# Four attentions in a two-block transformer: the product of the values ahead of the turn of the next probabilities

## The reference, cut to what matters

```python
s = q @ k.T * scale + mask         # 128 x (128, 256 or 512) scores
p = softmax(s, axis=-1)            # maximum, exp, sum, division
o = p @ v                          # 128 values (64 in the dilated one)
```

## Time and profile before

| | us |
|---|---|
| median of 3 runs | 1654.51 |
| lowest and highest run | 1649.87, 1654.61 |
| the profiled execution, its own time | 1649.54 |
| its span | 1647.8 |
| PE busy in it | 1546.7 (94%) |
| DVE, ACT busy | 1133.9 (69%), 796.8 (48%) |

### The profile page before, as it was taken

How to read it: one execution, slowest core, us unless ns; L and a number is a source line. 1 busy time by engine, 2 the same in 40 slices (tenths; PEclk the granted TensorE clock), 3 DMA queues, 4 the chain that set the end, 5 groups by cost and what they waited for, 6 DMA issues and landing times.

```text
span 1647.8 us, 31024 instructions
## 1 busy us (share of the span) xinstructions
PE 1546.7 (94%) x11438; PEld 1364.2 (83%) x11438; DVE 1133.9 (69%) x1901; ACT 796.8 (48%) x1437; POOL 124.6 (8%) x139
## 2 busy tenths in 40 slices
PE   5899988899899999999899999999999889999998
PEld 3688878888677777788786699999898669999997
DVE  5976866554799999867545468885665765577654
ACT  3545553242544444422355457774445455566532
POOL 2000152512000000001000010001000001000000
PEclk9999999999899999999899999999899999999999
DMA  9345510002255555554342035556454214255552
GB/s 364 112 174 179 187 46 1 3 2 77 96 186 180 189 185 184 178 179 153 118 148 77 1 128 191 180 195 212 152 167 141 90 65 130 89 192 187 183 191 89
DMA packets 62955, 230.77 MB, mean 140 GB/s; under 512 B 6800, under 2 KB 8080, under 8 KB 62352
## 3 DMA queue, kind: packets, MB, share of 16 engines
q1 hardware_dynamic: 61408, 223.37, 40.1%
q0 software_dynamic: 1168, 5.80, 1.0%
q10 hardware_dynamic: 288, 0.33, 0.1%
HBM read 228.43 MB, written 1.05 MB: 139 GB/s over the span
## 4 chain that ended last, share of the span: by engine, by line
PE 80%; DVE 11%; ACT 4%; issue 3%; POOL 1%; DMA 1%; DVEq 0%; ACTq 0%; POOLq 0%
PE proj L646 22%; PE proj L648 21%; PE proj L647 21%; DVE w_low L2138 2%; PE bank L698 1%; PE bank L900 1%; ACT w_high L1625 1%; PE bank L920 1%; PE bank L917 1%; DVE conv_mid L2218 1%; DMA ident_sb<-ident 1%; PE proj L1122 1%; DVE h_low L2171 1%; DVE tmp L2182 1%; PE bank L706 1%
## 5 line engine op out<-in xcount | busy, mean ns | idle before, releaser
L646 PE MATMUL proj<-h_high,w_high 128*128 128x256 f32 (+1 forms) x1776 | 584.7, 329 | 24.6 <-DVE h_low L2171 14.5
L648 PE MATMUL proj<-h_high,w_low 128*128 128x256 f32 (+1 forms) x1776 | 571.3, 322 | 0.0
L647 PE MATMUL proj<-h_low,w_high 128*128 128x256 f32 (+1 forms) x1776 | 570.4, 321 | 0.0
L2138 DVE TENSOR_TENSOR w_low<-w_raw,w_high 128x1024 fp32r<-128x1024 f32 x322 | 393.5, 1225 | 178.2 <-ACT w_high L1625 177.1
L1625 ACT ACTIVATE w_high<-w_raw 128x1024 fp32r<-128x1024 f32 x322 | 338.2, 1054 | 231.8 <-PE proj L648 227.5
L646 PEld LDWEIGHTS proj<-h_high,w_high 128*128 128x128 f32 x1776 | 336.8, 190 | 67.7 <-issue 19.1
L648 PEld LDWEIGHTS proj<-h_high,w_low 128*128 128x128 f32 x1776 | 337.2, 190 | 26.9
L647 PEld LDWEIGHTS proj<-h_low,w_high 128*128 128x128 f32 x1776 | 337.0, 190 | 24.6
L646 PE MATMUL proj<-act_high,w_high 128*128 128x256 f32 (+1 forms) x608 | 190.4, 313 | 0.4 <-DVE w_low L2138 0.4
L648 PE MATMUL proj<-act_high,w_low 128*128 128x256 f32 (+1 forms) x608 | 189.6, 312 | 0.0
L647 PE MATMUL proj<-act_low,w_high 128*128 128x256 f32 (+1 forms) x608 | 188.9, 311 | 0.0
(11 more groups left out here) (408 smaller groups left out, 1890.1 us busy)
## 6 DMA issues: line engine op xcount, KB each, us to landing
w_raw<-w_stream SPq DMA_DIRECT2D x322, 512.0 KB, 3.3
a_ring<-a_stream SPq DMA_DIRECT2D x80, 512.0 KB, 3.2
a_first<-a_head SPq DMA_DIRECT2D x4, 1024.0 KB, 18.1
a_first<-a_stream SPq DMA_DIRECT2D x4, 1024.0 KB, 18.6
x<-x_in SPq DMA_DIRECT2D x1, 2048.0 KB, 10.5
late_tab<-late_tables POOLq DMA_DIRECT2D x1, 1408.0 KB, 6.8
cond_rows<-cond_rows SPq DMA_DIRECT2D x1, 1024.0 KB, 5.9
cond_rows<-cond_rows POOLq DMA_DIRECT2D x1, 1024.0 KB, 5.2
```

Source lines behind the costliest of these rows:

```text
L646: mm(out_, wh, xh, start=first, stop=False)
L647: mm(out_, wh, xl, start=False, stop=False)
L648: return mm(out_, wl, xh, start=False, stop=last)
L2138: v.tensor_tensor(wl(n), RAW[:, n % 4, :], wh(n), ALU.subtract).then_inc(w_low, 1)
```

## The change

In both functions that write PE's part of an attention step, the block of the product with the values (of step a - 3) now stands ahead of the block of the turn (of step a - 2). Nothing else is altered: each block keeps its waits and its signals, and the lists of ACT, DVE, POOL and SP are the same as before. With the lines moved, the turn has the numbers L1172 and L1204 in the new kernel.

```diff
--- before.py
+++ after.py
@@ -1157,12 +1157,6 @@
                         elif ly is not MLA:
                             pe.wait_ge(A["at_p"], ly.a0 + max(0, a - nb + 1))
                             scores(a // 2, a % 2, ly.banks[a % nb]).then_inc(A["at_s"], 1)
-                    if 2 <= a < ly.n + 2:
-                        p = a - 2
-                        pe.wait_ge(A["at_n"], ly.a0 + p + 1)
-                        for k in range(ly.kt):
-                            last = nc.tensor.transpose(BK[2 + p % 2][:, k * P:(k + 1) * P], PB[:, p % 3, k * P:(k + 1) * P], ID[:])
-                        last.then_inc(A["at_t"], 1)
                     if a >= 3:
                         p = a - 3
                         pe.wait_ge(A["at_pt"], ly.a0 + p + 1)
@@ -1171,6 +1165,12 @@
                             pe.wait_ge(A["at_y"], ly.e0 + e - 1)
                         h, qt = (p // 4 * 2 + p % 2, p // 2 % 2) if ly is MLA else (p // 2, p % 2)
                         values(h, qt, PT[:, p % 2, :, :]).then_inc(A["at_o"], 1)
+                    if 2 <= a < ly.n + 2:
+                        p = a - 2
+                        pe.wait_ge(A["at_n"], ly.a0 + p + 1)
+                        for k in range(ly.kt):
+                            last = nc.tensor.transpose(BK[2 + p % 2][:, k * P:(k + 1) * P], PB[:, p % 3, k * P:(k + 1) * P], ID[:])
+                        last.then_inc(A["at_t"], 1)
 
             def pair_step(ly, a, scores, values):
 
@@ -1180,15 +1180,6 @@
                     for i in range(2):
                         last = scores(ly.pairs[a // 2][i], a % 2, BK[a % 2][:, i * SEQ:i * SEQ + (1 + a % 2) * P])
                     last.then_inc(A["at_s"], 1)
-                if 2 <= a < ly.n + 2:
-                    p = a - 2
-                    nk = 1 + p % 2
-                    pe.wait_ge(A["at_n"], ly.a0 + p + 1)
-                    for i in range(2):
-                        for k in range(nk):
-                            at = i * SEQ + k * P
-                            last = nc.tensor.transpose(BK[2 + p % 2][:, (i * nk + k) * P:(i * nk + k + 1) * P], PB[:, p % 3, at:at + P], ID[:])
-                    last.then_inc(A["at_t"], 1)
                 if 3 <= a < ly.n + 3:
                     p = a - 3
                     e, nk = p // 2, 1 + p % 2
@@ -1203,6 +1194,15 @@
                     for i in range(2):
                         last = values(ly.pairs[e][i], p % 2, PT[:, p % 2, i * nk:(i + 1) * nk, :], nk)
                     last.then_inc(A["at_o"], 1)
+                if 2 <= a < ly.n + 2:
+                    p = a - 2
+                    nk = 1 + p % 2
+                    pe.wait_ge(A["at_n"], ly.a0 + p + 1)
+                    for i in range(2):
+                        for k in range(nk):
+                            at = i * SEQ + k * P
+                            last = nc.tensor.transpose(BK[2 + p % 2][:, (i * nk + k) * P:(i * nk + k + 1) * P], PB[:, p % 3, at:at + P], ID[:])
+                    last.then_inc(A["at_t"], 1)
 
             def mla_scores(a, banks):
                 h, qt = a // 4 * 2, a // 2 % 2
```

## The result

The new order makes the kernel slower, by a little more than forecast: median 1658.08 us (1654.72 to 1664.67, 21 runs) against 1651.7 us for the kernel before on the same chip (1649.87 to 1655.97, 21 runs), a ratio of 1.0039 with a 95% interval of 1.0031 to 1.0047. As a difference that is +6.4 us; the forecast was +4.8.

The account below looks back on a forecast made before the run. PE was taken to bound the first attention (busy 46.64 of 49.0 us), DVE and ACT the dilated one. 4.7 - 0.6 - 0.2 + 0.9 = +4.8 us on the median of 1654.5 gave 1659.3 us, range 1652 to 1663.

Parts of the forecast that it names:

- The mechanism: In each step the product fills the wait for DVE's division, but may itself wait for ACT's copy of its turn.
- First attention, +4.7: First, latent attention: ten idle waits of 0.95 us for the copy come, nine division waits of 4.7 us go; +4.7 us.
- Dilated, -0.6: Dilated attention: DVE and ACT keep the pace; only the last wait counts, a 0.58 us product fits in; -0.6 us.
- Sparse, -0.2: Sparse attention: a wait of 0.65 goes in the first pair, about 0.45 is given back at the end; -0.2 us.
- Cross, +0.9: Cross attention: three copy waits of 0.69 in the last steps, 2.1 us, against 1.2 us of waits gone; +0.9 us.
- The sum: All four attentions together: 4.7 - 0.6 - 0.2 + 0.9 = +4.8 us.
- slower by over 0.3%: Whole kernel: slower by more than 5.0 us, chance 0.42, from 0.27 of the forecast's own and 0.15 for falling clock.
- First rival, the clock falls in the first attention: First attention: PE's clock falls to 1.2 GHz for some new waits; two falls add 3.6 us, 1662.9 us; chance 0.15.
- Second rival, faster: All four attentions: copies are never late, the product fills the division waits; -9.4 us, 1645.1 us; chance 0.08.
- Third rival, no change: Loss taken back behind the first attention, or sparse gains at their bound of -2.9; 1654.5 us; chance 0.17.

Follow-up runs that it names:

- e3: The changed kernel with ACT's copy of the first attention's turned probabilities made twice, one behind the other: 1663.04 us, ratio 1.0071 to the kernel before.
- e4: The kernel before with ACT's copy of the first attention's turned probabilities made twice: 1652.87 us, ratio 1.0001.
- e5: The kernel before, but in the first attention the product of a step earlier (a - 4) stands ahead of the turn: 1651.0 us, ratio 0.9994.
- e7: Kernel before with first attention's product a step later, ahead of the turn; new order in dilated and, but for its last three steps, sparse: 1650.3 us, ratio 0.9989.
- e6: The kernel before with the new order in the cross attention alone: 1651.23 us, ratio 1.0002.

## Why the prediction was right, and where it was not

- **The mechanism.** Right. The wait for the division goes and one for the copy comes, and the copy is the longer. e3, e4 and e5 show it: the time follows the copy's duration ten times over in the new order, and the loss is gone when another product stands there.
- **First attention, +4.7.** The sign and the ten waits were right (0.95 each forecast, 0.93 by the rows), the term was too small: +5.6. The step that was mis-sized is the length of a turn. The forecast took 0.39 for every turn, from turns that PE had stood idle ahead of the earlier trace rows; right behind a product it is 0.44, and in the new order 15 of the 16 turns stand so. A pair with two such turns grew by 0.70 instead of 0.60, and in all 15 times 0.05 make 0.75 of the 0.9 that lacked. The other 0.15 is as much as the same lengths missed the end of before by. The turn at 909.08 in the earlier trace rows stands behind a product too, but with an idle wait between, and showed 0.39.
- **Dilated, -0.6.** Right at -0.7, by the mechanism forecast: DVE's pace unchanged, PE's product ahead of its wait. The 0.58 was not the whole of the product's place: from the last turn to the block behind it is 1.17 us before (1328.39 to 1329.56) and 0.39 after (1338.60 to 1338.99). It depends on the clock there, as e7 shows.
- **Sparse, -0.2.** -0.5 was measured in every trace that has the new order throughout there. Two of the terms were right: the first pair gained 0.6, and the end gave 0.5 back. The two pairs behind the first were put at no gain, and each became 0.18 shorter (5.50 to 5.32 and 5.49 to 5.31 us, from their first scores to L1321). The two waits ahead of L1321, 0.61 each, came as forecast. Of the two waits for a copy the forecast had only the last; the other, 0.92 at 1366.59, stands with the second 0.61 where 1.54 for the division had been.
- **Cross, +0.9.** +1.1 (e6 and after): three waits of 0.71 for 0.69, and the turns behind products of 0.25 to 0.26 for 0.20 to 0.22.
- **The sum.** +4.8 forecast; +5.5 by the attentions' lengths, +6.4 by the medians, with an interval of +5.1 to +7.8, in which +5.5 lies. 0.9 us beyond the attentions was not found as a place. The first attention alone gave 1.005, again on the high side, but its six runs were at a lower clock than those beside them (0.9728 and 0.9743), and e3, with the whole new order, fits its lengths. 0.9 us is what 0.0008 of clock costs by the estimate above; for the runs of the changed kernel itself no clock is on record, so its source stays open. In absolute time the forecast of 1659.3 was close to the 1658.1 for a poorer reason: the median of three runs on which it was put was 2.8 us above that of 21 runs, and the change 1.6 us below what it proved to be.
- **The chances.** The measured interval begins at 1.0031, so the case is "slower by over 0.3%", to which the prediction gave 0.42 against 0.50 for no measurable change. The forecast divided its own range at 5.0 us, and the 0.75 us of the turns would have put its middle above it.
- **First rival, the clock falls in the first attention.** Wrong: it is 1.00 there in the changed kernel, with ten waits of 0.93. Where it did fall, it fell with either order. The prediction took a rule against waits in every second step from the Trainium skill (TensorE: Matmul & The Clock Gate, section HAM oscillation), and that reading was too wide: in the kernel that the section tells of, each wait is longer than the burst of about 2 us before it. Waits of 0.93 us, one in 6.59, are no test of that.
- **Second rival, faster.** Wrong but in the dilated attention, the one that has a block of a projection between turn and product, as the prediction said. The sparse one gained too, but 0.5 and not 2.9.
- **Third rival, no change.** Wrong: nothing behind the first attention gave the 5.6 us back.

## What to carry to other kernels

In a pipeline whose middle stage goes through another engine (turn on PE, copy on ACT, product on PE), what matters for PE's order is how much of its own work lies between the turn and the product that needs it. Removing the wait that the trace shows before a block is only half the sum; put the next dependency's latency, from the producer's start to the consumer's start, against the work that is left between them, and do it also for the last steps, where the work in between runs out. If a block is to stand first, take the one of a step earlier: it costs no instruction, only a longer end.

## What was not expected of the hardware

A turn of four 128x128 blocks takes 0.44 us to the next block right behind a product, and 0.39 where PE's loads had stood idle ahead of it, be it behind a product or behind the scores of the first attention with their idle 0.76. (The rows themselves are 0.47 and 0.42 long, and with two blocks 0.25 to 0.26 and 0.20 to 0.22.) Why was not looked into.

Behind the idle 1.8 us that PE spends ahead of the product with `ones` (L698) the clock either stays or falls, in the same program text. The loads there, of the kernel before and then of the changed one:

```profile
1243.72 0.52 PEld L698 LDWEIGHTS bank<-ones,tmp 128*128 128x128 f32 x4 [1.79 <-ACT tmp L1641]
```

```profile
1250.72 0.88 PEld L698 LDWEIGHTS bank<-ones,tmp 128*128 128x128 f32 x4 [1.80 <-ACT tmp L1641]
```

The waits are equal, 1.79 and 1.80, and both times PE had worked through its products without a gap before them. The products of 512 columns behind them follow one another every 0.43 us in the second and every 0.23 in the first. That is worth about 4 us a run, more than most edits here move. It is a part of why two single traces of this kernel can differ by 9 us with almost the same instructions, as before and e6 do: 3.7 of their 9.2, while 4.6 lie ahead of the first attention, where the clock over 200 to 300 us is 0.97 in the one and 0.93 in the other.
